# Layer-norm statistics of a two-layer decoder: narrow sums with a broadcast back, or wide sums that land on every partition

## What is computed

```python
def layer_norm(x, g, b):
    mu = jnp.mean(xf, axis=-1, keepdims=True)
    var = jnp.mean(jnp.square(xf - mu), axis=-1, keepdims=True)
    y = (xf - mu) * lax.rsqrt(var + EPS)
    return y * g + b

for l in range(DEPTH):
    x = layer_norm(ALPHA * x + 0.5 * swiglu(x, ffn1_w_in[l], ffn1_w_out[l]), ...)   # norm 0
    x = layer_norm(ALPHA * x + hybrid_mixer(x, ...), ...)                          # norm 1
    x = layer_norm(ALPHA * x + memory_cross_attn(x, mem, ...), ...)                # norm 2
    x = layer_norm(ALPHA * x + 0.5 * swiglu(x, ffn2_w_in[l], ffn2_w_out[l]), ...)   # norm 3
```

## Time and profile before

| | |
|---|---|
| median of 3 runs | 2417.15 us (2414.73 to 2418.87) |
| the profiled execution, own time | 2410.53 us |
| its span | 2408.3 us |
| TensorE matmul busy | 2273.0 us (94%), 10280 records |
| VectorE busy | 1113.8 us (46%) |
| ScalarE busy | 778.7 us (32%) |
| GpSimd busy | 1036.3 us (43%) |
| HBM read | 209.42 MB, 88 GB/s over the span |

### The profile page before, as it was taken

How to read it: one execution, slowest core, us unless ns; L and a number is a source line. 1 busy time by engine, 2 the same in 40 slices (tenths; PEclk the granted TensorE clock), 3 DMA queues, 4 the chain that set the end, 5 groups by cost and what they waited for, 6 DMA issues and landing times.

```text
span 2408.3 us, 25104 instructions
## 1 busy us (share of the span) xinstructions
PE 2273.0 (94%) x10280; PEld 1873.4 (78%) x10280; DVE 1113.8 (46%) x1137; ACT 778.7 (32%) x1017; POOL 1036.3 (43%) x434
## 2 busy tenths in 40 slices
PE   7999998968999899999899999989789998999996
PEld 6888887856878788888788888877568887888885
DVE  2333335787654633323343333359876455333333
ACT  3222223625443422222242222245344433222223
POOL 5444444414462444444354444443245525444441
PEclk9999998978999899999999999989789998999997
DMA  4333322211341233332223332222113312333320
GB/s 161 98 99 103 104 88 64 91 39 55 96 136 46 69 105 96 97 113 95 72 89 97 96 109 96 83 70 70 48 66 105 123 57 66 97 97 98 112 96 35
DMA packets 54113, 213.13 MB, mean 88 GB/s; under 512 B 6000, under 2 KB 6256, under 8 KB 53744
## 3 DMA queue, kind: packets, MB, share of 16 engines
q1 hardware_dynamic: 52704, 207.64, 26.7%
q10 hardware_dynamic: 1296, 3.90, 0.4%
HBM read 209.42 MB, written 2.10 MB: 88 GB/s over the span
## 4 chain that ended last, share of the span: by engine, by line
PE 85%; DVE 8%; ACT 2%; POOL 2%; DVEq 1%; issue 1%; ACTq 1%; DMA 0%; POOLq 0%
PE psum L429 24%; PE psum L430 24%; PE psum L433 24%; DVE tmp L1309 4%; PE psum L465 3%; PE psum L487 1%; PE psum L469 1%; POOL w_lo L341 1%; PE psum L511 1%; ACTq L893 1%; PE psum L409 1%; ACT w_hi L838 1%; PE psum L410 1%; PE psum L411 1%; PE psum L654 1%
## 5 line engine op out<-in xcount | busy, mean ns | idle before, releaser
L341 POOL TENSOR_TENSOR w_lo<-raw,w_hi 128x1024 fp32r<-128x1024 f32 (+3 forms) x356 | 937.2, 2635 | 1255.5 <-ACT w_hi L838 1255.4
L838 ACT ACTIVATE w_hi<-raw 128x1024 fp32r<-128x1024 f32 (+3 forms) x356 | 401.2, 1127 | 1388.5 <-PE psum L433 1264.5
L429 PE MATMUL psum<-act_hi,w_hi 128*128 128x512 f32 x1836 | 726.0, 395 | 41.5 <-ACT w_hi L838 41.5
L430 PE MATMUL psum<-act_lo,w_hi 128*128 128x512 f32 x1836 | 721.6, 393 | 0.0
L433 PE MATMUL psum<-act_hi,w_lo 128*128 128x512 f32 x1836 | 453.9, 389 | 0.0
L429 PEld LDWEIGHTS psum<-act_hi,w_hi 128*128 128x128 f32 x1836 | 349.2, 190 | 121.7 <-issue 42.5
L430 PEld LDWEIGHTS psum<-act_lo,w_hi 128*128 128x128 f32 x1836 | 349.6, 190 | 73.4 <-issue 0.5
L433 PEld LDWEIGHTS psum<-act_hi,w_lo 128*128 128x128 f32 x1836 | 344.7, 188 | 72.1
L1233 DVE TENSOR_TENSOR work<-work,psum 128x512 f32<-128x512 f32 x88 | 60.5, 688 | 614.9 <-PE psum L433 566.7
L429 PE MATMUL psum<-h_hi,w_hi 128*128 128x512 f32 x704 | 275.7, 392 | 0.0
L430 PE MATMUL psum<-h_lo,w_hi 128*128 128x512 f32 x704 | 275.5, 391 | 0.0
(11 more groups left out here) (227 smaller groups left out, 2101.4 us busy)
## 6 DMA issues: line engine op xcount, KB each, us to landing
raw<-w_in SPq DMA_DIRECT2D x176, 512.0 KB, 3.5
raw<-w_out SPq DMA_DIRECT2D x64, 704.0 KB, 4.0
raw<-w_mix SPq DMA_DIRECT2D x36, 512.0 KB, 3.5
raw<-w_kv SPq DMA_DIRECT2D x32, 512.0 KB, 3.5
raw<-w_mixout SPq DMA_DIRECT2D x16, 576.0 KB, 3.8
raw<-w_q SPq DMA_DIRECT2D x16, 512.0 KB, 3.5
raw<-w_o SPq DMA_DIRECT2D x16, 512.0 KB, 3.5
raw<-w_v SPq DMA_DIRECT2D x4, 768.0 KB, 4.2
```

The lines of the kernel that those rows point to most:

```text
L341: nc.gpsimd.tensor_tensor(w_lo[:, r, 0:width], raw[:, j, 0:width], w_hi[:, r, 0:width].bitcast(F32), ALU.subtract).then_inc(slot_split, 1)
L429: nc.tensor.matmul(o, hi, b_hi, start=start and k == 0, stop=False)
L430: nc.tensor.matmul(o, hi, b_lo, start=False, stop=False)
L838: A(w_hi[:, place % SPLIT, 0:width], raw[:, place, 0:width], ACT.Copy).then_inc(w_hi_made, 1)
```

## The change

The sums' stationary operand is now 1/1024 on a whole 128x128 block, and the data are the moving operand, 512 wide: mean and mean square land on all partitions, in banks 6 and 7, and no broadcast follows. ScalarE squares the mean; VectorE forms variance + eps on 128x512; ScalarE takes Abs_reciprocal_sqrt of it into bank 4; VectorE centres tiles 0 and 1 meanwhile, then does a Newton step in three passes, leaves the scale in bank 5, and multiplies each centred tile by it. The affine and rounding stay.

With it come smaller edits. The first two slots of a layer are rounded by ScalarE and split by GpSimd like all others, across the layer's border too. The table for the root is loaded before the residual tiles, the silu table behind the eighth rounding of norms 0, 2 and 3. In norm 1 the key read 2 now stands between the mean square and the root. The decay rates move to pairs 4 and 5, VectorE's part behind pair 5. The last norm rounds nothing, and its stores wait for the affine. Semaphore counts start at zero instead of a head start.

```diff
-        average = consts[:, C_AVG:C_AVG + 1]
+        average = consts[:, C_AVG:C_AVG + 1].to_broadcast([P, P])
+        mean, square_mean, first_root, scale = bank(6), bank(7), bank(4), bank(5)
...
             def stats(layer, n):
...
-                def total(a, source, before):
-                    for t in range(TT):
-                        last = nc.tensor.matmul(psum[:, 6, a * TT + t:a * TT + t + 1],
-                                                source[:, t * P:(t + 1) * P], average,
-                                                ...
+                pe.wait_ge(z_summed, sum_count(layer, n, KT - 2))
+                nc.tensor.matmul(mean, average, zsum, start=True, stop=False)
+                nc.tensor.matmul(square_mean, average, zsqsum, start=True, stop=False)
+                pe.wait_ge(z_added, z_count(layer, n, KT - 1))
+                nc.tensor.matmul(mean, average, x[:, KT - 1, :], start=False, stop=True)
+                pe.wait_ge(z_squared, z_count(layer, n, KT - 1))
+                nc.tensor.matmul(square_mean, average, zsq(KT - 1), start=False,
+                                 stop=True).then_inc(stats_ready, 1)
-            def bcast(layer, n):
...
@@ ScalarE
+            def w_hi_of(n):
+                if n >= SPLIT:
+                    act.wait_ge(slot_multiplied, n - SPLIT + 1)
+                if n < TOTAL:
+                    act.wait_ge(raw_loaded[n % RAW], (n // RAW + 1) * 16)
+                    width = slot_width(n % SLOTS)
+                    A(w_hi[:, n % SPLIT, 0:width], raw[:, n % RAW, 0:width],
+                      ACT.Copy).then_inc(w_hi_made, 1)
...
+            w_hi_of(0)
+            w_hi_of(1)
             for k in range(KT):
                 act.wait_ge(x_loaded[k // 2], 16)
                 A(act_hi[:, k, :], x[:, k, :], ACT.Copy).then_inc(x_hi_made, 1)
...
+            def square_of_mean(layer, n):
+                act.wait_ge(stats_ready, group(layer, n))
+                A(var[:, :], mean, ACT.Square).then_inc(mean_squared, 1)
             def root(layer, n):
-                act.wait_ge(var_ready, layer * 4 + n + 1)
-                A(small[:, 16:20], small[:, 12:16], ACT.Sqrt).then_inc(std_ready, 1)
-                if n >= 2:
-                    A(small[:, 46:47], small[:, 47:48], ACT.Silu)
+                act.wait_ge(var_ready, group(layer, n))
+                A(first_root, var[:, :], ACT.Abs_reciprocal_sqrt).then_inc(root_ready, 1)
+            def scaled(layer, n, k):
+                act.wait_ge(y_centered, x_count(layer, n, k) - KT)
+                last = A(x[:, k, :], x[:, k, :], ACT.Identity, bias=vec(c + 8), scale=vec(c))
+                if n == 3 and layer == LAYERS - 1:
+                    last.then_inc(x_finished, 1)
+                    return
                 act.drain()
                 A(act_hi[:, k, :], x[:, k, :], ACT.Copy).then_inc(x_hi_made, 1)
+            def normed(layer, n):
+                square_of_mean(layer, n)
+                root(layer, n)
+                for k in range(KT):
+                    scaled(layer, n, k)
+                silu_table()
...
                 read_k(0)
                 read_k(1)
+                square_of_mean(layer, 1)
+                read_k(2)
                 root(layer, 1)
-                read_k(2)
...
@@ VectorE
             def norm(layer, n, eps):
-                ...
+                def centered(k):
+                    V.tensor_tensor(x[:, k, :], x[:, k, :], mean, ALU.subtract)
+                v = var[:, :]
+                dve.wait_ge(mean_squared, group(layer, n))
+                V.tensor_tensor(v, square_mean, v, ALU.subtract)
+                dve.drain()
+                V.tensor_scalar(v, v, 0.0, eps, ALU.max, ALU.add).then_inc(var_ready, 1)
+                for k in range(2):
+                    centered(k)
+                dve.wait_ge(root_ready, group(layer, n))
+                V.scalar_tensor_tensor(v, v, -0.5, first_root, ALU.mult, ALU.mult)
+                dve.drain()
+                V.tensor_tensor(v, v, first_root, ALU.mult)
+                dve.drain()
+                V.scalar_tensor_tensor(scale, v, 1.5, first_root, ALU.add, ALU.mult)
                 for k in range(KT):
-                    V.tensor_tensor(x[:, k, :], x[:, k, :], bank(4), ALU.mult)
+                    if k >= 2:
+                        centered(k)
                     dve.drain()
-                    V.tensor_tensor(x[:, k, :], x[:, k, :], bank(5),
-                                    ALU.subtract).then_inc(y_centered, 1)
+                    V.tensor_tensor(x[:, k, :], x[:, k, :], scale, ALU.mult).then_inc(y_centered, 1)
```

More of the change, by code:

```diff
@@ L71, in slot_width, with z_count, sum_count, group @@
     return KT * P
+TOTAL = LAYERS * SLOTS
+def z_count(layer, n, part):
+    return layer * 4 * KT + n * KT + part + 1
+def sum_count(layer, n, m):
+    return layer * 4 * (KT - 1) + n * (KT - 1) + m + 1
+def group(layer, n):
+    return layer * 4 + n + 1
+def x_count(layer, n, k):
+    return KT + layer * 4 * KT + n * KT + k + 1
 V_LN = 0
@@ L324, in _ @@
                 stage(w_out2, layer, S_OUT[1], 16, 11 * P)
[L325 to L329, removed]
+            for k in range(0, KT, 2):
+                sp.wait_ge(x_finished, k + 2)
+                sp.dma_start(out[:, k:k + 2, :], x[:, k:k + 2, :]).then_inc(out_stored, 16)
             sp.wait_ge(out_stored, 64)
@@ L368, in split_x @@
                                             ALU.subtract).then_inc(x_split, 1)
[L370 to L380, removed]
@@ L716, in attention @@
                 stats(layer, 1)
-                k_tile(2)
-                bcast(layer, 1)
-                for m in range(3, KT):
+                for m in range(2, KT):
                     k_tile(m)
@@ L908, in ffn @@
-                squares(layer, n, S_OUT[f], 2)
-                root(layer, n)
-                for k in range(KT):
-                    affine(layer, n, k)
+                s0 = layer * SLOTS + S_IN[f]
+                for i in range(FT):
+                    w_hi_of(s0 + 2 * i + SPLIT)
+                    if i >= 2:
+                        act.wait_ge(h_made, base + i - 1)
+                    A(work[:, i % 2, :], bank(2 * (i % 2)), ACT.Silu).then_inc(gate_silu, 1)
+                    w_hi_of(s0 + 2 * i + 1 + SPLIT)
+                    if f == 0 and i in (4, 5):
+                        decay_rates(layer, i - 4)
@@ L913, in decay_rates @@
+                root_table()
+                s0 = layer * SLOTS + S_OUT[f]
+                for m in range(KT):
+                    for r in range(2):
+                        w_hi_of(s0 + 2 * m + r + SPLIT)
+                    square(layer, n, m)
+                normed(layer, n)
             def decay_rates(layer, part):
@@ L1121, in attention @@
                 context(XH - 1)
-                squares(layer, 2, S_AO, 1)
-                root(layer, 2)
-                for k in range(KT):
-                    affine(layer, 2, k)
+                root_table()
+                for m in range(KT):
+                    step(layer, S_AO + m)
+                    square(layer, 2, m)
+                normed(layer, 2)
             for layer in range(0, LAYERS):
@@ L1239, in ffn @@
-                if f == 0:
-                    decay_rates(layer)
+                for i in range(FT):
+                    h, hi, lo = work[:, 2 + i % 2, :], h_hi[:, i, :], h_lo[:, i, :]
+                    done(layer, S_IN[f] + 2 * i + 1)
+                    dve.wait_ge(gate_silu, base + i + 1)
+                    V.tensor_tensor(h, work[:, i % 2, :], bank(2 * (i % 2) + 1),
+                                    ALU.mult).then_inc(h_made, 1)
+                    dve.drain()
+                    V.tensor_copy(hi, h)
+                    dve.drain()
+                    V.tensor_tensor(lo, h, hi.bitcast(F32), ALU.subtract).then_inc(h_split, 1)
+                    if f == 0 and i == 5:
+                        decay_rates(layer)
```

360 lines of the change are left out of this document (123 added, 237 removed).

## The result

The changed kernel takes 2386.76 us (median of 4 runs, 2385.05 to 2387.26); the kernel before, on the same chip, 2415.94 us (4 runs, 2413.63 to 2418.87). The ratio is 0.9877, with a 95% interval of 0.986 to 0.9894: 29.2 us faster.

The account below looks back on a forecast made before the run. TensorE, 85% of the chain, was taken to bound the kernel, with gains only where it stands still. 3.56 + 10.65 - 1.1 + 0 + 1.0 + 4.5 = 18.6 us off the median 2417.15 gave 2398.5; range 2390 to 2410.

Parts of the forecast that it names:

- The sums: Layer norm sums as four wide fp32 matmuls: 3.45 us each, 3.56 us won over the five exposed norms.
- rival (b): In the norms' sums: the clock falls to its lower level, 3.4 us more each, 2419 us in all; chance 0.03.
- From the sums to the first matmul: In the five exposed norms, from the sums' end to the next stage: 7.65 us instead of 9.78, 10.65 won.
- rival (c): VectorE's passes in six norms: a flush after each makes every norm 2.65 us longer, 2414.5 in all; chance 0.02.
- Tables: ScalarE's loads of root and silu tables stay covered and cost nothing; if uncovered, 1.5 us per norm.
- rival (a): In six norms: a 1.28 us table load falls between mean square and root, 5 us less won, 2403.5; chance 0.07.
- The clock behind a norm: TensorE's slow restart after the five exposed norms: 1.1 us lost, bounds 3.2 lost and as much won.
- Norm 1: Beside cross-attention's key tiles, both layers: ScalarE's first affine starts when it did, so 0 us; bounds 3.5 won, 2.7 lost per layer.
- Start and end: First two weight slots shared by ScalarE and GpSimd: 1.0 us won; last norm to span end: 22.2 us, 4.5 won.
- the first one: Whole kernel: TensorE is 85% of the chain, mostly untouched weight matmuls, so gains come only where TensorE stands still.
- the last step of the sum: Whole kernel: 2391.9 us from the profiled execution, raised to 2398.5 because that execution was 6.6 below the median.
- The range: Whole kernel: 2390 to 2410 us, from some 8 us down and 11 up.

Follow-up runs that it names:

- a_nonewton: The changed kernel without the three Newton passes, the first root used as the scale; 2368.0 us, ratio 0.9803 to the kernel before.
- a_rootfirst: The changed kernel with norm 1's root on ScalarE moved ahead of key read 2; 2384.28 us, ratio 0.9869 to the kernel before.
- a_shift64: The changed kernel with 64 unused bytes a partition ahead of the large region; 2392.94 us, ratio 0.9907 to the kernel before.
- b_same: The kernel before with 1472 bytes a partition of padding, so its hidden tiles lie at the changed kernel's addresses; 2405.7 us against 2417.77, ratio 0.995.
- b_same_again: A repeat of b_same, the kernel before with 1472 bytes of padding; 2403.72 us against 2416.49, ratio 0.9951.

## Why the forecast was right in its steps and wrong in its number

**The sums.** 3.43 to 3.44 us in every exposed norm where 3.45 was worked out, and at the full clock throughout; rival (b) did not occur.

**From the sums to the first matmul.** 55.99 us for five norms where 5 x 11.1 = 55.5 was forecast: 13.73 won of the 14.21 in these two terms. The passes stood where the working put them (5.25 us from the sums to the first product, forecast 5.28); the 0.5 missing lies in two norms of layer 0, 0.36 and 0.28 longer than the other three; in norm 0 it is the clamp, issued that much later behind the pass before it. a_nonewton confirms that each Newton pass is on the path. Against rival (c) and the rule it rests on, of the Trainium skill, VectorE: DVE Perf Modes, section "The DRAIN you can't avoid", the passes start at 381.81, 382.57 and 383.33, 0.76 us apart and not 1.11. (The section excepts a next operation that is not held back, so it is less strict than the prediction made it; but the flush of 0.42 us that its figure gives for a pass of 0.69, an estimate, does not appear here even with an explicit drain between the passes.)

**Tables.** No load falls on the path; rival (a) did not occur. The silu table is loaded behind the eighth rounding, the next activation 0.02 us behind its end, in ScalarE's trace after:

```profile
396.20 1.28 ACT L831 ACT_TABLE_LOAD   x1
397.50 0.20 ACT L831 ACTIVATE small<-small 128x1 f32<-128x1 f32 x1
```

**The clock behind a norm.** Charged with 1.1 us lost, it gave some: 19.82 us at the lower level instead of 21.48, 0.8 us won. The comparison with one stretch behind a longer stand was a poor guide; single norms vary from 3.07 to 5.68 without order.

**Norm 1.** The first affine starts 7.78 us behind the end of the sums (642.80 to 650.58), the working said 7.75. Keys and norm 1 took 26.79 us in both layers, where they took 26.77 and 26.76. The charge of 0 was right, and a_rootfirst shows the reason given for it, the root's place in ScalarE's queue.

**Start and end.** First matmul at 11.97 instead of 12.62: 0.65 won, 1.0 forecast, as the slot landed later than assumed (its rounding starts at 8.39). End: 22.16 us, forecast 22.2.

Together these terms give 13.73 + 0.8 + 0 + 0.65 + 4.59 = 19.8 us. The smaller edits had no runs of their own; that the decay rates cost nothing in their new place is seen in the 223.04 us of the FFN's slots in both traces.

The step that failed is the first one, by which "almost all of the TensorE share is weight matmuls that this change leaves alone, so it can only win where TensorE stands still". The change moves their operands. That was worth 4.7 us in the FFN-out slots and 1.3 in the values and cross-attention, 6.0 together (a_shift64: 6.2 by the medians). Without it the time would have been inside the range: a_shift64 took 2392.94.

The mixer's sparse part, 3.0 us longer, gives some of it back. In the trace the loss stands where the clock is low; the same 16 matmul records in layer 0, after and then before (the granted clock is the third number from the end):

```profile
560.86:565.30 4.44, 4.44 (x16) 3.37 (x16) 4.29 (x4) 1.32 (x3) 0.00 (x0) 0.50 0.00 0
```

```profile
565.26:567.80 2.54, 2.54 (x16) 1.98 (x16) 2.47 (x2) 1.00 (x3) 0.00 (x0) 1.00 0.00 0
```

Whether the change has a part in it is not settled. In layer 0 one and the same program took 91.97 us in b_same and 93.61 in b_same_again. But in layer 1 the four profiles of the kernel before and its padded forms took 91.8 to 92.0 us, the nine with the new norm 92.2 to 95.5. With this the account stands at 19.8 + 6.0 - 3.0 = 22.8 of the 23.8 us between the two spans; about 1 us, behind the start and in the mixer's dense part, is not traced to a cause. The terms of the forecast sum to 18.6, and that the change by itself then measured 18.9 and 17.0 is in part luck, as the mixer's 3.0 offset a gain of more than was forecast.

A second error lies in the last step of the sum. The profiled execution before was 6.6 us under its median, and the forecast carried this over to the kernel after, whose profiled execution (2386.35) is at its own median. Profile against profile the gain is 24.2 us, and the other 5 appear only in the medians: with the kernel before's addresses went its lower mean clock, 0.957. b_same shows this twice for the kernel before; a_shift64 shows that in the kernel after the old distance does not bring the lower clock back. Why the addresses move the clock, and in which stage, stays open.

The range had an error of its own. Its lower end counts the clock's 4.3 us (1.1 lost to 3.2 won) and 3.5 for norm 1, "some 8 us"; but the 3.5 was a bound for each layer, and with both the sum is 11.3 and the range would have begun near 2387.

## What to carry to other kernels

Before pricing an edit, write down the addresses of all operands before and after it: a new tile moves everything allocated behind it, and the distance between a matmul's two operands can change its pace by 1 to 3% over stages that the edit never names. To measure an edit by itself, pad one of the kernels until the addresses agree. Where a profiled execution lies several us off its own median, compare the granted clocks of single runs before carrying the difference over.

## What the runs showed of the hardware that was not expected

- A slot of 33 matmuls 128x512 takes 7.48, 7.55 or 7.70 us, one of 24 takes 5.44 or 5.60, at a granted clock of 1.0 and with no wait, by the distance in SBUF of stationary and moving operand (modulo 512, of the distances tried: 0 or 256; 64; 128 or -64).
- The mean granted clock of one program, the kernel before, moved from 0.957 to 0.960 with padding alone, repeatably (41 runs against 20). In the kernel after, 64 B of padding did not lower it (0.968 to 0.969 against 0.967 to 0.968).
- A VectorE pass with one operand in PSUM keeps its 0.68 us beside a GpSimd subtraction; one from SBUF to SBUF grows from 0.43 to 0.93 in the median. The Trainium skill, SBUF — State Buffer, section "Who interferes with whom", tells of a pair of ports that the two engines share and take in turn; this agrees, by those two numbers.
- 32 needless matmuls in each exposed norm pay: 6.5 us less, as TensorE then returns to work at 2.4 GHz.
